# The last two expert passes interleaved: both up products, then both down products, in the loads and in the matrix work

## What is computed

```
logits = t @ w_router + b_router            # t: 256 tokens x 1024, after RMSNorm
gates  = softmax of the 4 largest logits, 0 elsewhere
for e in range(32):
    act = clamped_swiglu(t @ w_up[e] + b_up[e])           # w_up[e]: 1024 x 2048
    out = out + gates[:, e:e+1] * (act @ w_down[e] + b_down[e])   # w_down[e]: 1024 x 1024
return rmsnorm(x + out, final_g)
```

## Time and profile before

| What | us |
|---|---|
| median of three executions | 1093.94 |
| lowest and highest | 1092.67, 1095.78 |
| the profiled execution, its own time | 1092.85 |
| its span, first to last instruction | 1090.9 |
| TensorE busy in the span | 1025.4 (94%) |
| VectorE busy | 249.3 (23%) |
| ScalarE busy | 105.9 (10%) |
| granted TensorE clock, mean | 0.982 |
| read from HBM | 428.17 MB |

### The profile page before, as it was taken

How to read it: one execution, slowest core, us unless ns; L and a number is a source line. 1 busy time by engine, 2 the same in 40 slices (tenths; PEclk the granted TensorE clock), 3 DMA queues, 4 the chain that set the end, 5 groups by cost and what they waited for, 6 DMA issues and landing times.

```text
span 1090.9 us, 11415 instructions
## 1 busy us (share of the span) xinstructions
PE 1025.4 (94%) x4936; PEld 485.6 (45%) x4936; DVE 249.3 (23%) x581; ACT 105.9 (10%) x238; POOL 21.6 (2%) x28
## 2 busy tenths in 40 slices
PE   9999999999999998999989898989999989999887
PEld 8888886333333333333333333333333333333332
DVE  2322123312131212120303112121212130303022
ACT  2131012101010100000000001010000000000002
POOL 2100002000000000000000000000000000000001
PEclk9999999999999999999999999999999998999999
DMA  9804995999999999999999999999999999999995
GB/s 336 308 1 154 425 384 222 425 431 434 427 419 433 428 433 428 433 430 431 431 432 431 429 434 428 433 430 431 431 430 434 428 424 430 428 426 430 425 419 200
DMA packets 36271, 429.99 MB, mean 394 GB/s; under 512 B 5835, under 2 KB 7548, under 8 KB 19068
## 3 DMA queue, kind: packets, MB, share of 16 engines
q1 hardware_dynamic: 31760, 427.04, 92.7%
q10 hardware_dynamic: 4156, 1.14, 0.5%
q0 software_dynamic: 304, 1.06, 0.3%
HBM read 428.17 MB, written 1.06 MB: 393 GB/s over the span
## 4 chain that ended last, share of the span: by engine, by line
PE 76%; DMA 20%; issue 2%; ACT 1%; DVE 1%; POOL 0%; SPq 0%; ACTq 0%; DVEq 0%; POOLq 0%
PE bank L1038 28%; PE bank L1118 21%; DMA ring<-in_w_down 16%; PE bank L777 9%; PE bank L1016 5%; PE bank L967 4%; DMA ring<-in_w_up 3%; PE bank L885 3%; PE bank L996 1%; PE bank L791 1%; PE bank L1006 1%; ACT h_buf L686 1%; PE bank L745 0%; PE bank L922 0%; PE bank L801 0%
## 5 line engine op out<-in xcount | busy, mean ns | idle before, releaser
L1038 PE MATMUL bank<-ring,z_buf 128*64 128x512 f32 x2048 | 450.5, 595 | 13.5 <-issue 12.8
L1038 PEld LDWEIGHTS bank<-ring,z_buf 128*64 128x64 f32 x2048 | 147.3, 137 | 299.5 <-issue 299.3
L1118 PE MATMUL bank<-ring,h_buf 128*64 128x512 f32 x1024 | 242.3, 629 | 39.1 <-DMA ring<-in_w_down 28.3
L1118 PEld LDWEIGHTS bank<-ring,h_buf 128*64 128x64 f32 x1024 | 78.8, 144 | 181.5 <-issue 166.1
L1461 DVE COPY y<-bank 128x256 f32<-128x256 f32 x32 | 12.1, 419 | 287.8 <-PE bank L1118 287.8
L777 PE MATMUL bank<-h_buf,ring 128*128 128x256 f32 x336 | 75.7, 380 | 0.0
L967 PEld LDWEIGHTS bank<-u_buf,m_buf 128*128 128x128 f32 x512 | 59.7, 192 | 22.8 <-issue 22.7
L777 PEld LDWEIGHTS bank<-h_buf,ring 128*128 128x128 f32 x336 | 63.6, 190 | 8.7 <-issue 0.2
L967 PE MATMUL bank<-u_buf,m_buf 128*128 128x128 f32 x512 | 65.5, 281 | 0.0
L1411 DVE TENSOR_TENSOR z_buf<-bank,g2x 128x512 f32<-128x512 f32 (+1 forms) x33 | 22.3, 675 | 166.5 <-PE bank L967 165.3
L1446 DVE TENSOR_SCALAR swi<-bank 128x256 f32<-128x256 f32 x62 | 26.3, 424 | 136.1 <-PE bank L1038 131.3
(11 more groups left out here) (196 smaller groups left out, 402.9 us busy)
## 6 DMA issues: line engine op xcount, KB each, us to landing
ring<-in_w_up SPq DMA_DIRECT2D x44, 4096.0 KB, 24.3
ring<-in_w_down SPq DMA_DIRECT2D x22, 4096.0 KB, 22.2
ring<-in_w_up SPq DMA_DIRECT2D x34, 2048.0 KB, 28.2
ring<-in_w_down SPq DMA_DIRECT2D x14, 2048.0 KB, 28.6
ring<-in_w_up SPq DMA_DIRECT2D x12, 1024.0 KB, 10.5
ring<-in_w_in SPq DMA_DIRECT2D x5, 2048.0 KB, 22.5
ring<-in_w_down SPq DMA_DIRECT2D x10, 1024.0 KB, 30.1
ring<-in_w_out SPq DMA_DIRECT2D x2, 2048.0 KB, 17.3
```

The costliest lines, as they stand in the source:

```text
L1038: ins = nc.tensor.matmul(up_banks[j][e * SLOTS:(e + 1) * SLOTS, :], xgT[:, k, e * SLOTS:(e + 1) * SLOTS], w[e].rearrange("p (k n) -> p k n ...
L1118: ins = nc.tensor.matmul(down_banks[n][e * SLOTS:(e + 1) * SLOTS, :], hidT[:, k, e * SLOTS:(e + 1) * SLOTS], w[e], start=(k == 0), stop=(k ...
```

## The change

Passes 0 to 13 stay as they are. For passes 14 and 15 the order of the loads, of the ring's slots, and of the products becomes: up 14, up 15, down 14, down 15. A function `position(g, i)` gives a load its place, and `wait_freed` looks ten places back in that order. So down 14 is now loads 184 to 187, and up 15 is 176 to 183. On PE:

- both halves of the gather for pass 15 and its bias come right behind up 14, ahead of up 15;
- both turns of pass 14 come there as well;
- down 14 comes behind up 15, its two rows in one go;
- then turn of half 0 of pass 15, the four scatters of pass 14, turn of half 1, down 15, and the last scatters.

The loads of row kk = 3 of pass 15 and those of down 14 are whole. Row m = 0 of down 15 stays in halves. Row m = 1 now comes in whole rows: k = 4 and 5, then k = 6, and then k = 7 in two halves of its columns. PE does k = 4, 5, 6 for both halves of the columns, and then k = 7 for the one and the other. The last y1 copy is waited for as a whole, and its two scatters are no longer cut in two.

On ACT the copy of y0 of pass 14 moves behind the four sigmoids of pass 15. On DVE the copy of y1 of pass 14 moves behind the clips of pass 15, and the second gathered half of pass 15 ahead of them. `final_g` waits for `cols_done` of the last pass.

```diff
+def position(g, i):
+    if g < LAST - 1:
+        return g * LOADS + i
+    begin, later = (LAST - 1) * LOADS, g - (LAST - 1)
+    if i < UP_LOADS:
+        return begin + later * UP_LOADS + i
+    return begin + 2 * UP_LOADS + later * (LOADS - UP_LOADS) + i - UP_LOADS
...
-                back = load - R
-                if back < 0:
-                    back, g = back + LOADS, g - 1
+                g, back = ORDER[position(g, load) - R]
...
-            def load_tail(n):
-                src = w_down_d[2 * LAST:2 * LAST + 2, CH:2 * CH, n * CH:(n + 1) * CH].rearrange("e (p k) n -> p e k n", p=P)
-                dst = ring[:, slot_of(LAST * LOADS + LOADS - 2 + n), :].rearrange("p (e k n) -> p e k n", e=2, n=CH)
-                parts = [slice(0, 4)] if n == 0 else [slice(0, 2), slice(2, 4)]
-                for i, ks in enumerate(parts):
+            def load_tail():
+                src = w_down_d[2 * LAST:2 * LAST + 2, CH:2 * CH, :].rearrange("e (p k) n -> p e k n", p=P)
+                pieces = [(slice(0, 2), slice(0, D)), (slice(2, 3), slice(0, D)), (slice(3, 4), slice(0, CH)), (slice(3, 4), slice(CH, D))]
+                for (ks, cols), landed in zip(pieces, tail_landed):
                     for e in range(2):
-                        sp.dma_start(dst[:, e, ks, :], src[:, e, ks, :]).then_inc(tail_landed[n + i], 16)
+                        dst = ring[:, slot_of(LAST, LOADS - 2 + e), :].rearrange("p (k n) -> p k n", n=D)
+                        sp.dma_start(dst[:, ks, cols], src[:, e, ks, cols]).then_inc(landed, 16)
...
+            def pe_down(g, slot_load, turn=None, first=False):
+                pe.wait_ge(hidT_copied, g * MH + 1)
+                pe.wait_ge(spreadT_copied, g + (1 if turn else 2))
+                w = [slot_load(UP_LOADS + e) for e in range(2)]
+                if turn is None:
+                    pe.wait_ge(hidT_copied, g * MH + 2)
...
+            def pe_down_last(g):
+                pe.wait_ge(hidT_copied, g * MH + 2)
+                pe.wait_ge(spreadT_copied, g + 1)
...
+                for k in (4, 5, 6):
+                    if k != 5:
+                        pe.wait_ge(tail_landed[(k - 3) // 2], 32)
+                    for n in range(2):
+                        down(k, n, w)
+                for n in range(2):
+                    pe.wait_ge(tail_landed[2 + n], 32)
+                    ins = down(7, n, w)
+                    ins.then_inc((down0_done, down_done)[n], 1)
...
+            def pe_last_two(loads):
+                a, b = LAST - 1, LAST
+                pe_up(a, loads[0], later=True)
+                gather(b, 0, 4, gather_bank, gather_done)
+                turn_hid(a, 0, False)
+                turn_hid(a, 1, False)
+                gather_second(b)
+                up_bias(b)
+                pe_up(b, loads[1], last=True)
+                pe_down(a, loads[0])
+                turn_hid(b, 0, False)
+                for q in range(4):
+                    pe.wait_ge(lin_ready, b * NJ + q + 1)
+                    scatter(a, q, late=True)
+                turn_hid(b, 1, False)
+                pe_down_last(b)
+                for q in range(4):
+                    scatter(b, q, last=True)
```

More of the change, by code:

```diff
@@ L94, in count_landed @@
     at = {}
[L95 to L104, removed]
+    for g, i in ORDER:
+        slot = (EXPERTS_AT + position(g, i)) % R
+        if (g, i) in IN_PARTS:
+            continue
+        if in_pairs(g) and i % 2:
+            at[g, i] = at[g, i - 1]
+        else:
+            loads[slot] += 1
+            at[g, i] = slot, loads[slot]
     return at, loads
@@ L456, in _ @@
                     sp.wait_ge(w_out0_done, 1)
-                load_expert(slot_of(load), load, FIRST)
-            for g in range(PASSES):
+                load_expert(slot_of(FIRST, load), load, FIRST)
+            for g in range(LAST - 1):
                 for load in range(R if g == FIRST else 0, LOADS):
@@ L1100, in pe_pass @@
                     pe.wait_ge(bias_added, 2)
+            def pe_down(g, slot_load, turn=None, first=False):
[4 more added lines that the diff above has]
+                    pe.wait_ge(hidT_copied, g * MH + 2)
+                for k in range(4):
+                    for n in range(2):
+                        ins = down(k, n, w)
+                ins.then_inc(down_done, 1)
+                if turn is not None:
+                    turn()
+                    pe.wait_ge(hidT_copied, g * MH + 2)
+                if first:
+                    for h in range(2):
+                        pe.wait_ge(early_landed[h], 32)
+                    w = [ring[:, slot_of(g, LOADS - 2 + e), :] for e in range(2)]
+                else:
+                    w = [slot_load(UP_LOADS + 2 + e) for e in range(2)]
+                for n in range(2):
+                    for k in range(4, 8):
+                        ins = down(k, n, w)
+                    ins.then_inc((down0_done, down_done)[n], 1)
@@ L1101, in pe_pass @@
+            def pe_pass(g, slot_load, following, first=False, second=False, pairs=False, biased=False, later=False):
+                pe_up(g, slot_load, first, second, biased, later)
                 if following and pairs:
                     gather(g + 1, 0, 4, gather_bank, gather_done)
[L1103 to L1104 removed]
                 turn_hid(g, 0, pairs)
@@ L1436, in prepare, with copy_y1 @@
                 build_spread(g + 1, g + 1)
+            def copy_y1(g):
+                dve.wait_ge(down_done, g * MH + MH)
+                for i in range(2):
+                    part = slice(i * CF, (i + 1) * CF)
+                    nc.vector.tensor_copy(y[:, CH + part.start:CH + part.stop], down_banks[1][:, part]).then_inc(y1_copied, 1)
             def dve_pass(g, following, last=False):
@@ L1456, in dve_pass @@
                     copy_xg(g + 1, 0, gather_bank)
-                def copy_y1():
-                    dve.wait_ge(down_done, g * MH + MH)
-                    for i in range(2):
-                        part = slice(i * CF, (i + 1) * CF)
-                        nc.vector.tensor_copy(y[:, CH + part.start:CH + part.stop], down_banks[1][:, part]).then_inc(y1_copied, 1)
+                if following and g + 1 == LAST:
+                    copy_xg(g + 1, 1, gather_bank)
+                    return
                 if last:
+                    copy_y1(g - 1)
                     for q in range(4):
```

206 lines of the change are left out of this document (83 added, 123 removed).

## The result

| | kernel before | changed kernel |
|---|---|---|
| median of 20 executions, us | 1093.24 | 1095.63 |
| lowest, highest | 1091.82, 1095.78 | 1094.56, 1098.21 |
| ratio of the times, 95% interval | 1 | 1.0024 [1.0018, 1.003] |
| profiled execution: time, span | 1092.85, 1090.9 | 1095.04, 1093.1 |

The changed kernel is 2.4 us slower by the medians, and its ratio is 1.0024: clear of the noise and small. The forecast was 2.9 us slower, 0.26%.

What follows compares the result with a forecast made beforehand. PE's own backlog behind one landing was taken as the bound: 1056.75 + 7.0 + 5.43 + 13.88 = 1083.06 beside 1079.71, +3.3 to +3.4 us. This gave 1096.2 or 1097.3; 1096.8 was taken, range 1094.5 to 1099.0.

Steps and rivals of the forecast that it cites:

- What bounds the end: End of the last two passes: PE's own backlog behind one landing sets it, not the last byte; before, 32.74 us.
- critical row: Row m = 1 of down 14 in the changed kernel, started by load 187's landing; 7.0 us on the path.
- Load 187 at 1056.75: Second expert's load for row m = 1 of pass 14 lands at 1056.75, one beat of 9.78 us after 1046.97.
- a start before 1056: Sign of a wrong prediction: row m = 1 of pass 14 starting before 1056, where 1056.75 was forecast.
- The terms behind it: After load 187: down 14 row 7.0 us, turns and scatters 5.43, down 15 13.88, ending at 1083.06.
- The waits of PE: PE waits ahead of kk = 3 of pass 15 and both rows of down 14, 2.4 to 2.8 us each.
- What lies hidden: At the end: y0 copy and table hidden with 0.3 us to spare; y1 copy and last row's cut cost zero.
- The allowance for the clock: Sum of +3.3 to +3.4 us was taken as +2.9 on the median; the clock risk before may cancel.
- critical stretch: Kernel before, from the landing at 1046.97 to the last scatters at 1079.71: 32.74 us of work.
- The number: Whole kernel: 1096.8 us, +2.9 us or 0.26% on the median of three, 1093.94.
- The rival of the clock: Clock falls at load 187's row, adding 1.7 us: 1098.5 us, slower by more than 0.3%; chance 0.26.

Runs made afterwards that it cites:

- the one with the full dose: Changed kernel with 16, 20 and 20 identity products ahead of row kk = 3 of pass 15 and both rows of down 14: 1101.10 us, ratio 1.0075.
- the new tail alone: Kernel before with only the new cut of the last row, its product order and y1 waited for whole; pass order unchanged: 1093.50 us, ratio 0.9998.
- the pair of tails with a held clock: Changed kernel with 8, 10 and 10 identity products ahead of three waits, last row in four pieces or two: 1095.94 and 1096.13 us.
- The pair with held clocks: Kernel before with 10 identity products ahead of row kk = 2 of pass 15, and changed kernel with 8, 10 and 10: 1092.52 and 1095.94 us.
- three variants of the changed order: Changed kernel with pass 14 scatters cut to 2 columns, scatter q = 3 behind the second turn, or last row in two pieces: 1094.51, 1095.14, 1096.99 us.
- the kernel with the finest cut: Kernel before with new tail, finer loads for up 15 rows kk = 2 and 3, and last-row k = 4 and 5 in separate pieces: 1090.85 us, ratio 0.9978.
- the one with the finer up loads: Kernel before with new tail, up 15 row kk = 2 in halves, kk = 3 as k = 6 and two column halves of k = 7: 1092.00 us, ratio 0.9989.

## Why the prediction was right

*What bounds the end.* Right. A critical row that started 6.0 us later moved the last scatters by 6.0 us; holding the clock or changing the tail did not take the loss away.

*Load 187 at 1056.75.* In the profile of the changed kernel the row starts at 1055.88, in the others of this order, but for the one with the full dose, at 1056.2 to 1057.1. The prediction named a start before 1056 as a sign of being wrong, and by 0.1 us that sign came. It does not count against the mechanism: PE still waited 0.93 us for the landing. Where the stream stands differs by about a microsecond from one execution to the next. In this one it was 0.9 us early, and that is most of why the spans differ by 2.2 us and not by 3.3.

*The terms behind it.* 7.0 + 5.43 + 13.88 = 26.3 us were computed; 7.09, 5.26 and 13.95 stand in the chain, 26.3 in all. Down 15 so started at 1068.2 instead of 1069.2 and the last scatters at 1082.2 instead of 1083.1, early by about the same 0.9 us.

*The waits of PE.* I expected 2.4 us ahead of kk = 3 and 2.8 ahead of both rows of down 14. They were 0.95, 2.81 and 0.93: the fall at kk = 2, behind a wait of 2.00 us that I had not counted among the risky ones, ate the next wait, and the fall at row m = 0 ate the last.

*What lies hidden.* y0, y1 and the table cost nothing, as said, by the profile. The cut of the last row cost nothing by two runs, the new tail alone and the pair of tails with a held clock.

*The allowance for the clock.* I took 0.4 to 0.5 us off, since the risk "may cancel". The pair with held clocks would put it at 3.4 - 2.4 = 1.0 us in the medians, from the side of before: it pays for falls at its single wait in the critical stretch. That is likely and not shown, since the difference is within the intervals, and the changed order did not get faster when its clock was held.

*The number.* The forecast of 1096.8 us was 1.2 us too high. 0.7 us of that is the start: the median of three executions was 1093.94 us, and that of 20 is 1093.24. The other 0.5 us is the difference, 2.9 forecast and 2.4 measured. A miss so small is partly luck, since one execution differs from the next by more.

*The rival of the clock.* It did occur: the profiles of three variants of the changed order show the fall at the critical row. They show something else too. There the falls stand at kk = 3 and at m = 1, behind waits of 2.4 and 2.6 us. In the changed kernel's own profile they stand at kk = 2 and at m = 0. A slow row makes the next wait short, and the row behind a short wait was fast each time, so in these four profiles every second row is slow, and whether kk = 2 has a fall decides whether the critical row has one. The executions of the changed kernel near 1098 us may be of the first kind. That its median is not is argued from the held clock, which did not lower it, and is not shown.

## What to carry to other kernels

Find the last landing that the chain starts from, and compare what stands behind it on both sides: rows of work on the engine, rows of loads in the queue. A reordering that trades one row for the other moves the end by the difference. Finer loads paid where the engine waited at the start of that backlog, in part perhaps through the clock, and only once that wait was gone did they pay at the tail. Latency that other work has filled is no gain when it is moved off the path: ask first how long the stretch would be with the work alone.

## What the runs showed of the hardware

- Cutting four products to 2 columns in a stretch that was bound by other engines made the kernel 1.7 us slower: PE was busy for 2.63 of 4.80 us, and the granted clock then stood at 0.53 for 3.4 us of the next stretch. The Trainium skill (TensorE: Matmul & The Clock Gate, HAM oscillation) says that waits for DMA between bursts of products bring the slow clock back. This trace shows a fall behind waits for POOL and ACT too, of 0.36, 1.16 and 0.65 us, each shorter than the waits of that section's kernel. So short fillers can be worth more than their time.
- Waits of 2.0 and 2.8 us were followed by the lower level in the profile of the changed kernel, one of 2.67 us was not in the profile of before and was in another one of the same order (15.65 us for the product instead of 13.95). One of 1.95 us was (the row at 1016.57 in the kernel with the finest cut, 8.78 us), and one of 2.97 us was not (the row at 1017.66 in the one with the finer up loads, 7.09 us). The length alone does not tell.
- A product of the identity, 128 x 128 in float32, took 0.236 us. With 8 to 20 of them ahead of each wait that they were to guard, the clock was 1.00 from 1044 to 1083 in each of the profiles taken so.
- DMAs of 256 and 512 KB at the end of the stream cost it nothing that can be seen in the times: the kernel with the finest cut is the fastest, and the new tail alone has a ratio of 0.9998 [0.9989, 1.0007].
